# A two-layer block on one core: the gating unit's bias put into each bank first, and heads of a pair side by side in mixing and pooling

## The reference

```
# pooling, 4 groups of 64 columns, windows 2, 4, 8, 16
win_sum / cnt - pg[:, :, g]          # a fixed 256 x 256 matrix per group
# gating unit, 4 heads of 64 columns, chunks of 128 tokens
mixed = einsum('hpq,bcqhd->bcphd', sgu_w, vc) + sgu_b.T[None, None, :, :, None]
return u * mixed
```

## Time and profile before

| | |
|---|---|
| median of 3 runs | 2056.79 us |
| lowest and highest | 2055.26 and 2058.39 us |
| span of the profiled execution (first to last instruction) | 2050.1 us |
| PE busy | 1990.1 us, 97% of the span |
| DVE busy | 1195.2 us, 58% |
| ACT busy | 890.0 us, 43% |
| mean DMA rate | 155 GB/s |

### The profile page before, as it was taken

One profiled execution on the slowest core, in us unless ns is written; L12 is line 12 of the kernel. 1 busy time (PEld: TensorE's weight loads), 2 busy tenths in 40 slices (PEclk: granted clock), 3 DMA queues, 4 the chain that ended last, 5 costly groups with the idle time before them and its releaser, 6 DMA issues.

```text
span 2050.1 us, 33804 instructions
## 1 busy us (share of the span) xinstructions
PE 1990.1 (97%) x13960; PEld 1728.6 (84%) x13960; DVE 1195.2 (58%) x2137; ACT 890.0 (43%) x1514; POOL 167.0 (8%) x187
## 2 busy tenths in 40 slices
PE   7899999999999999999999999999999999999998
PEld 7768999897889999787788877777778897997887
DVE  6756666776466666425434455444444635677776
ACT  5656544436464444325423333222232426455443
POOL 0220100012021100003410000000000003000000
PEclk9999999999999999899999999999999999999999
DMA  7374699856656665225433325455444421664554
GB/s 233 100 225 146 182 224 224 213 173 188 203 153 180 187 209 164 62 59 163 129 102 93 104 72 185 144 183 165 151 144 153 136 77 37 188 193 144 185 185 134
DMA packets 331751, 317.60 MB, mean 155 GB/s; under 512 B 17077, under 2 KB 315964, under 8 KB 331342
## 3 DMA queue, kind: packets, MB, share of 16 engines
q1 hardware_dynamic: 326580, 301.64, 48.3%
q0 software_dynamic: 3904, 12.03, 2.9%
q10 hardware_dynamic: 1114, 1.76, 0.3%
HBM read 306.54 MB, written 8.85 MB: 154 GB/s over the span
## 4 chain that ended last, share of the span: by engine, by line
PE 87%; DVE 6%; DMA 3%; ACT 2%; issue 1%; POOL 0%; ACTq 0%; SPq 0%; DVEq 0%; POOLq 0%
PE acc L673 20%; PE acc L674 19%; PE acc L675 19%; PE acc L723 7%; PE acc L722 4%; DVE w_low L1963 3%; PE pss L872 2%; PE acc L688 1%; PE acc L719 1%; PE acc L689 1%; PE acc L690 1%; DMA raw<-in_w_mod 1%; PE pst L884 1%; ACT w_high L1421 1%; DMA raw<-in_l_w_down 1%
## 5 line engine op out<-in xcount | busy, mean ns | idle before, releaser
L1963 DVE TENSOR_TENSOR w_low<-raw,w_high 128x1024 fp32r<-128x1024 f32 (+4 forms) x503 | 561.5, 1156 | 151.9 <-ACT w_high L1421 149.3
L1421 ACT ACTIVATE w_high<-raw 128x1024 fp32r<-128x1024 f32 (+4 forms) x503 | 471.9, 984 | 393.8 <-PE acc L675 242.7
L673 PE MATMUL acc<-normed,w_high 128*128 128x256 f32 (+1 forms) x1768 | 568.7, 322 | 0.2
L674 PE MATMUL acc<-normed,w_high 128*128 128x256 f32 (+1 forms) x1768 | 563.4, 319 | 0.0
L675 PE MATMUL acc<-normed,w_low 128*128 128x256 f32 (+1 forms) x1768 | 562.9, 318 | 0.0
L673 PEld LDWEIGHTS acc<-normed,w_high 128*128 128x128 f32 x1768 | 338.4, 191 | 28.7 <-issue 4.4
L675 PEld LDWEIGHTS acc<-normed,w_low 128*128 128x128 f32 x1768 | 338.5, 191 | 22.8
L674 PEld LDWEIGHTS acc<-normed,w_high 128*128 128x128 f32 x1768 | 338.6, 192 | 22.3
L723 PE MATMUL acc<-inner,w_high 128*128 128x512 f32 x612 | 218.1, 396 | 0.0
L673 PE MATMUL acc<-inner,w_high 128*128 128x512 f32 (+2 forms) x576 | 199.2, 346 | 2.2 <-DVE w_low L1963 2.0
L674 PE MATMUL acc<-inner,w_high 128*128 128x512 f32 (+2 forms) x576 | 196.7, 341 | 0.0
(11 more groups left out here) (278 smaller groups left out, 2783.6 us busy)
## 6 DMA issues: line engine op xcount, KB each, us to landing
raw<-in_w_ff SPq DMA_DIRECT2D x128, 512.0 KB, 4.3
raw<-in_w_mod SPq DMA_DIRECT2D x96, 512.0 KB, 4.8
raw<-in_w_in SPq DMA_DIRECT2D x84, 512.0 KB, 4.1
raw<-in_l_w_gate SPq DMA_DIRECT2D x44, 512.0 KB, 5.2
raw<-in_l_w_up SPq DMA_DIRECT2D x44, 512.0 KB, 4.4
raw<-in_l_w_down SPq DMA_DIRECT2D x32, 512.0 KB, 4.7
raw<-in_l_w_qkv SPq DMA_DIRECT2D x24, 512.0 KB, 4.4
raw<-in_l_w_out SPq DMA_DIRECT2D x16, 512.0 KB, 4.6
```

Of the source, the lines that this page charges most:

```text
L673: mm(dst, lh, rh, start=i == 0, stop=False)
L674: mm(dst, lh, rl, start=False, stop=False)
L1421: nc.scalar.activation(WH[:, s % NSPLIT, w0:w0 + nw], RAW[:, r:r + nw], ACT.Copy).then_inc(w_high, 1)
L1963: V.tensor_tensor(WL[:, s % NSPLIT, c], RAW[:, r:r + nw], WH[:, s % NSPLIT, c].bitcast(F32), ALU.subtract).then_inc(w_low, 1)
```

## The change

In pooling, the loops are reordered so that groups 0 and 1 (then 2 and 3) are issued in turn, one on each half. In gating, the sixteen matmuls of a bank (eight of a head, eight of the bias) become ten: first two with two rows each, one per half, which put the bias of two heads over all 512 columns of their half of the bank (the weights are a row of the identity spread over 64 columns, so that each half picks its own of the two bias rows), then eight for the heads, accumulating onto it, with the two halves in turn. The bias is loaded into two partitions of 256 numbers instead of one of 512, again by one DMA. Nothing else is changed.

```diff
--- before.py
+++ after.py
@@ -189,6 +189,8 @@
             return CST[0:rows, lo:hi]
 
         ident, ones = const("ident"), const("ones")
+        row_of_two = [bass.AP(tensor=ident.tensor, offset=ident.offset + e, ap=[[ident.ap[0][0], 2], [0, 64]])
+                      for e in range(2)]
 
         def view(t, base, shape, p0=0, p1=P):
 
@@ -274,7 +276,9 @@
         out_nat, out_gain = wk(0, NB, D), wk(2048, D)
         OUT_T = ((PSS[0], PSO), (PSS[1], PST))
         lines = wk(0, 2, 127, p1=120)
-        sgu_b = PT[0:1, 0, 0, :]
+        sgu_b = PT[0:2, 0, 0, 0:S]
+        sgu_rows = bass.AP(tensor=sgu_b.tensor, offset=sgu_b.offset,
+                           ap=[list(sgu_b.ap[0]), [P, 2], [0, NB], [1, P]])
         sgu_t = view(MASK, 0, (4, P))
         raw_sgu = view(MASK, 512, (4, P))
         wpool = view(MASK, 1024, (2, P))
@@ -1202,11 +1206,12 @@
                 pe.wait_ge(b2_in, 16 * 6 * (l + 1))
                 for s in range(T // S):
                     b = bank()
-                    for g in range(4):
-                        lo = 64 * (g % 2)
+                    for i in range(2):
                         for t in range(NB):
-                            ins = mm(b[lo:lo + 64, S * (g // 2):S * (g // 2) + S],
-                                     pn[:, NB * s + t, 64 * g:64 * g + 64], pool_a[:, t, g, :], start=t == 0, stop=t == 1)
+                            for e in range(2):
+                                g = 2 * i + e
+                                ins = mm(b[64 * e:64 * e + 64, S * i:S * i + S], pn[:, NB * s + t, 64 * g:64 * g + 64],
+                                         pool_a[:, t, g, :], start=t == 0, stop=t == 1)
                     ins.then_inc(acc_full, 1)
                 if l:
                     spread(S, at=S)
@@ -1220,14 +1225,14 @@
                 pe.wait_ge(ln_done, 4 if l == 0 else 6)
                 for s in range(T // S):
                     b = bank()
-                    for h in range(4):
-                        lo = 64 * (h % 2)
+                    for e in range(2):
+                        mm(b[64 * e:64 * e + 64, :], row_of_two[e], sgu_rows, start=True, stop=False)
+                    for i in range(2):
                         for c in range(NB):
-                            at = S * (h // 2) + P * c
-                            mm(b[lo:lo + 64, at:at + P], vs[:, NB * s + c, 64 * h:64 * h + 64], sgu_t[:, h, :],
-                               start=True, stop=False)
-                            ins = mm(b[lo:lo + 64, at:at + P], ones[0:1, 0:64], sgu_b[:, P * h:P * h + P],
-                                     start=False, stop=True)
+                            for e in range(2):
+                                h, at = 2 * i + e, S * i + P * c
+                                ins = mm(b[64 * e:64 * e + 64, at:at + P], vs[:, NB * s + c, 64 * h:64 * h + 64],
+                                         sgu_t[:, h, :], start=False, stop=i == 1 and c == NB - 1)
                     ins.then_inc(acc_full, 1)
                 st["store"] += 2 * (T // S) + (4 if l else 0)
                 for i in range(5):
@@ -2689,7 +2694,8 @@
                 for g in range(4):
                     lo = 64 * (g % 2)
                     sp.dma_start(wpool[lo:lo + 64, g // 2, lo:lo + 64], A["w_pool_2"][l, g]).then_inc(b2_in, 16)
-                sp.dma_start(sgu_b, A["sgu_b_2"][l:l + 1].rearrange("o h p -> o (h p)")).then_inc(b2_in, 16)
+                sp.dma_start(sgu_b.rearrange("e (i p) -> e i p", i=2),
+                             A["sgu_b_2"][l].rearrange("(i e) p -> e i p", e=2)).then_inc(b2_in, 16)
                 sp.dma_start(pool_a, A["pool_m"].rearrange("p (b g t) -> p b g t", b=NB, g=4)).then_inc(b2_in, 16)
 
             sp.dma_start(nat[0], rows("x")).then_inc(x_in, 16)
```

## The result

The changed kernel takes 2034.49 us, the median of 4 runs (2029.39 to 2036.90), against 2057.59 us (2055.26 to 2058.50) of the kernel before run beside it: a ratio of 0.9889, 95% interval 0.9871 to 0.9906, 23 us less. The prediction was 2035.3 us, between 2031 and 2041.

The account below looks back on a forecast made before the run. PE, holding 87% of the chain of waits, was taken as the bound. Savings of 16.7 + 2.8 + 1.9 + 0.1 = 21.5 us took 2056.8 to 2035.3 us, range 2031 to 2041.

Parts of the forecast that it names:

- Pooling: Pooling matmuls: both halves already run together, so the new order saves 0.1 us over three banks, between 0 and 0.3.
- Heads: Gating's head matmuls: sixteen records in eight pairs cost 1.02 us a bank, as in the attention.
- Bias: Gating's two bias matmuls: 1.02 us a bank if side by side, 1.90 if not, 0.9 at the low end.
- The stage: Gating over three banks: 6.1 us where 22.85 stood, 16.7 us less.
- The clock behind it: Products behind gating speed up if the clock stays at 1.00: 2.8 us in the first layer, 1.9 in the second.
- Who waits next: Other engines behind PE: no new wait; second layer holds by 0.4 us or more, else up to about 1 us returns.
- The clock stayed up: Against the rival that gating's clock falls all the same: 2038.4 us once, 2041.5 in both layers; chance 10%.
- Pairing: Against the rival that gating's half-width matmuls don't pair: 2037.9 us for the bias, 2040.5 with heads too; chance 7%.
- The order of the halves: Rival in pooling: the old order kept the halves apart, so 6 us more would be gained, 2029 us; chance 1%.
- the accumulation onto one place: Rival in gating: 0.36 us comes from changing halves or accumulating, not row count; 2054 us; chance 1%.
- the stretch of 1219.4: A 6.8 us lower-clock stretch outside gating may vanish, or a like one appear, 3.1 us either way.
- The slower case: Rival in the attentions: after the shift the clock could fall there, eating 25.7 us to reach 2061; chance 2%.

Follow-up runs that it names:

- pool_order: The kernel before with only pooling's loops in the new order, gating untouched; 2054.59 us, ratio 1.0004 to the kernel before.
- one_row_first: The kernel before with each bank's eight one-row bias matmuls moved ahead of its eight head matmuls; 2034.15 us, ratio 0.9905.
- bias_on_dve: The changed kernel without bias matmuls, DVE adding the bias before it multiplies the bank; 2032.45 us, and 2029.38 us when run again.
- changed once more: The changed kernel, unaltered, run again as the reference for other runs; 2033.96 us, ratio 0.9897 to the kernel before.
- gate_alone: The changed kernel with pooling put back in its old order; 2033.83 us, ratio 0.9895 to the kernel before.
- all_rows_alt: The kernel before with each one-row bias matmul replaced by a 128-row one in the old alternation, bias left out of the result; 2035.02 us.
- alt_first: The changed kernel with heads and two-row bias matmuls alternating again in the first layer's two banks only; 2049.18 us.
- alt_one_bank: The changed kernel with heads and two-row bias matmuls alternating again in the first layer's first bank only; 2039.20 us.

## Why the prediction was right

**The bound.** PE was the chain before and after the earlier trace rows, and the 21.6 us that the two changed pieces lost reached the end: from the start of pooling to the end of the span it was 1203.3 us and is 1180.7, 22.6 less. The sizes, step by step:

- *Pooling*: 0.1 us forecast, 0.11 measured (3.73 to 3.67 and 2.00 to 1.95), and pool_order shows it alone. The reading that both halves ran together already, 0.12 us a record against 0.25, was the one that kept 6 us out of the sum.
- *Heads*: 1.02 us a bank, taken from the attention; measured 1.02. The split of a lone matmul's 0.36 us into 0.22 of streaming and 0.14 of filling and emptying holds too: the starts of its two records lie 0.16 us apart and the next matmul follows 0.20 later (852.40, 852.56, 852.76 in the kernel before), where records at full pace come every 0.11. Of the 0.23 us a matmul that the new order saves, about half is thus filling and emptying, and the rest is that the other half now streams alongside.
- *Bias*: 1.02 us, bounded by 0.9 and 1.90; measured 1.00, the two halves side by side. The row count by itself is indifferent: in one_row_first eight one-row matmuls take 1.07 us and eight of 128 rows 1.08.
- *The stage*: 16.7 us forecast; 22.85 became 4.05 and 2.03 (1622.47 to the start of the product at 1624.50), 16.8 less.
- *The clock behind it*: 2.8 and 1.9 forecast. By pieces, 14.95 less 12.02 for the stage and 0.06 for pooling leaves 2.9; 6.68 less 4.75 and 0.05 leaves 1.9.
- *Who waits next*: nobody, as forecast. The second layer's margin was undersized at 0.4 us. DVE took the gating bank at 1627.53, straight behind its normalising, and ended the split at 1632.91 + 2.36 = 1635.27; the third product came at 1636.79, right behind the rotation that starts at 1636.11. The margin was 1.5 us. I had set ACT's 2.00 and DVE's 2.36 us of a split end to end, and they overlap by 0.9 (1650.10 to 1652.10 on ACT, from 1651.18 on DVE in the kernel before). The expectation of bias_on_dve, written with 1.7, had it a little too large:

```profile
1627.53 0.68 DVE L2542 TENSOR_TENSOR probs_t<-acc,work 128x512 f32<-128x512 f32 x1
...
1632.91 2.36 DVE L1968 TENSOR_TENSOR w_low<-raw,w_high 128x1024 fp32r<-128x1024 f32 x2 [0.55 <-ACT w_high L1426]
```

**The rivals.** The clock stayed up in both stages; the forecast's argument, that half the new stage is work of the attention's kind, was not the full reason, since blocks of one- and two-row matmuls of 1.0 us, half of each stage, didn't bring it down either. That the clock stays up was read off the attention, and it held. Pairing held for the bias, which no row had shown. The order of the halves and the accumulation onto one place, behind two further rivals, were tested and are out. The remark that the stretch of 1219.4 may change came half true: it lasts 6.8 us in the kernel before and its counterpart 3.4 us in the changed one, from 1208.6 on, which would be worth 3.4 x (1 - 0.23/0.42) = 1.5 us over full work. No run tells whether the change did that: among the kernels with the new stages it lasts 3.4 us in some (changed once more) and 6.8 in others (gate_alone). The slower case did not appear in any of the changed kernel's eight runs.

**What was off.** The span: 2028.6 forecast, 2030.7 measured in an execution of 2032.5 us. The page and the run list of the profile after show that only 1.8 us lie around a span. The 6.7 us that I had carried over as constant were 1.8 us and a profiled execution that was quicker than the median by 4.9 us. Most likely that was in the part ahead of the change, since its pooling starts at 846.8 us and that of every other profile at 848.1 or later; the execution that gave the median was not profiled. In the difference of medians this cancelled. The remaining 1.6 us between 21.5 and the measured 23.1 are within the scatter of 4 runs each; the pieces fit the working to 0.1 us, and 1.0 us came outside them. That the forecast time itself lies within 1 us of the measured one is in part luck, at a scatter of 7 us.

The Trainium skill, "TensorEngine Tiling (Array Packing)", section "Key Properties", says that going from one tiling mode to another drains the engine and that going from tile to tile does not. The runs agree if a matmul of one or two rows is in another mode than one of 128, which no record names: 0.36 us a matmul when rows change between 128 and one or two, 0.13 to 0.16 when they don't, whichever half comes next.

## What to carry to other kernels

When PE is busy without a gap, compare starts, not busy time: 0.36 us for a 128-column matmul beside 0.13 for the same form elsewhere was the clue. Sort matmuls that share a bank by row count, all biases of a bank first, and let the halves pair by themselves; the interleaving is worth 0.06 us a bank here and the shape of the bias matmul 0.07. A stretch of such alternation can cost twice: one bank of it cost 3.7 us itself and 2.9 more through the lower clock, so count what runs at the lower clock behind it as part of its price.

## What was not expected

**The clock falls without idle time.** PE had no gap in the alternating stages (5.10 busy of 5.10 us), yet each of seven brought the clock from 1.00 to 0.50 within 3.9 to 5.1 us, and all_rows_alt, with just as many matmuls of the same columns in the same order, kept 1.00. What PE did before the clock fell was to start a matmul every 0.36 us with a change of row count each time; in all_rows_alt it started one every 0.14 without a change. Blocks of one-row matmuls ran at 1.00 too, but they last 1.1 us each, too short to say that one-row work alone keeps the clock up. Whether the pace or the switching itself matters, these runs can't tell apart. The Trainium skill, "TensorE: Matmul & The Clock Gate", section "HAM oscillation — how this bites in real kernels", looks for this in gaps in which PE waits for data; here it came in stages that the profile books as busy throughout. What exactly the chip counts was not measured.

**Half-width matmuls pass one another.** With all four records of one half issued before those of the other, they still run together: 3.73 us for 32 records against 3.67 in turn. PE's timeline of the kernel before, in windows so narrow that only two records are merged, shows it:

```profile
846.82 0.44 PE L1208 MATMUL acc<-work 128*64 128x256 f32 x2
847.09 0.39 PE L1208 MATMUL acc<-work 128*64 128x256 f32 x2
```

Two records together last 0.44 and 0.39 us, only 0.01 us more than one, so they start 0.01 us apart (further on starts 0.06 and 0.16 us apart alternate), and a pair comes every 0.22 us, the pace of the single full-width records behind them. Two records of one matmul never start so close: when alone they are 0.16 us apart. So the second of each pair must be the other half's, though the program issues it four records later. That it is picked out of the queue is what these starts say; the records themselves name no half.

**The runs scatter ahead of the change.** The same instructions reach the pooling of the first layer between 846.8 and 854.5 us of the span. The profiles show short stretches at clock 0.50 in that part in varying number, from one in the kernel before to five in alt_first. They can't be all of it: alt_one_bank has three of them and starts pooling at 854.4, later than alt_first with its five (851.9). What the rest is was not settled. It means that a single run of this kernel tells little under 7 us, while a piece of the timeline around the edit tells 0.1 us.
